# The end of layer 0 by tiles of 128 tokens

## What is computed

```python
for l in range(DEPTH):
    ...
    hl = rmsnorm(x, norm1_w[l]) * (1 + sc1) + sh1
    hc = rmsnorm(ctx, norm1_w[l]) * (1 + csc1) + csh1
    ...
    e_idx, e_w = route_hierarchical(toks, ...)      # two experts a token
    ffn = moe_ffn(toks, e_idx, e_w, w_gate, w_up, w_down)
    x = x + g2 * ffn[:n_lat].reshape(b, t, d)
    if not last:
        ctx = ctx + cg2 * ffn[n_lat:].reshape(ctx.shape)
```

## Time and profile before

| | us |
|---|---|
| median of 3 runs | 3706.56 |
| lowest, highest | 3702.25, 3714.03 |
| the profiled execution, device time | 3713.84 |
| its span, first to last instruction | 3711.9 |
| TensorE busy | 3456.7 (93%) |
| VectorE, ScalarE, Pool busy | 1631.2, 1048.9, 677.6 |
| mean granted TensorE clock | 0.978 of full |

### The profile page before, as it was taken

The page is one execution under the profiler, slowest core; times in us unless marked ns, Lnnn a source line. Parts: engine busy times, 40 slices in busy tenths (PEclk is TensorE's granted clock), DMA queues, the critical chain, the costliest instruction groups (busy, mean ns, idle before and its releaser), DMA issues. The chain is left out here.

```text
span 3711.9 us, 92740 instructions
## 1 busy us (share of the span) xinstructions
PE 3456.7 (93%) x41758; PEld 1938.9 (52%) x41758; DVE 1631.2 (44%) x2896; ACT 1048.9 (28%) x1844; POOL 677.6 (18%) x583
## 2 busy tenths in 40 slices
PE   6989999999999999999999597998999999999997
PEld 3454444545666666443332345656656666774333
DVE  3584803664766663221000356824256666531111
ACT  2211002504545543111111321104145555420001
POOL 0151200302434332010000002113033333300000
PEclk8999999999999999999999799999999999999998
DMA  5103622341110111359998211833311111268996
GB/s 203 64 5 108 221 68 80 120 136 41 27 36 23 28 34 48 115 205 421 404 393 343 101 46 46 260 113 103 93 27 36 26 31 31 53 225 369 424 424 272
DMA packets 255517, 538.69 MB, mean 145 GB/s; under 512 B 49520, under 2 KB 173696, under 8 KB 222224
## 3 DMA queue, kind: packets, MB, share of 16 engines
q1 hardware_dynamic: 236064, 463.98, 34.3%
q0 software_dynamic: 19056, 68.69, 5.3%
HBM read 514.75 MB, written 17.87 MB: 143 GB/s over the span
## 5 line engine op out<-in xcount | busy, mean ns | idle before, releaser
L1299 PE MATMUL banks<-sb_h,sb_ring 128*128 128x512 f32 (+1 forms) x1344 | 476.4, 513 | 10.1 <-DMA sb_ring<-w_branch 6.5
L1816 PEld LDWEIGHTS banks<-inv 64*64 64x64 f32 x15104 | 290.3, 134 | 170.6 <-issue 168.4
L1299 PEld LDWEIGHTS banks<-sb_h,sb_ring 128*128 128x128 f32 x1344 | 255.5, 191 | 224.0 <-issue 196.6
L1816 PE MATMUL banks<-inv 64*64 64x64 f32 x15104 | 328.5, 221 | 14.3 <-issue 10.6
L1825 PE MATMUL banks<-sb_h,sb_ring 128*128 128x512 f32 (+1 forms) x672 | 329.6, 598 | 6.2 <-DMA sb_ring<-w_in 4.1
L819 PE MATMUL banks<-sb_h,sb_ring 128*128 128x512 f32 x512 | 232.1, 611 | 19.4 <-SPq L241 19.4
L3189 PE MATMUL banks<-gu,xs 128*64 128x512 f32 x768 | 169.5, 594 | 5.1 <-DMA gu<-gu_pairs 4.6
L819 PEld LDWEIGHTS banks<-sb_h,sb_ring 128*128 128x128 f32 x512 | 99.8, 197 | 138.8 <-issue 118.1
L2533 DVE COPY inv<-banks 128x512 f32<-128x512 f32 x144 | 98.9, 691 | 164.9 <-PE banks L1816 164.1
L3341 DVE TENSOR_TENSOR hrow<-hrow,banks 128x256 f32<-128x256 f32 x36 | 15.1, 421 | 355.2 <-ACT hrow L3377 355.2
L1299 PE MATMUL banks<-sb_branch,sb_ring 128*128 128x512 f32 (+1 forms) x512 | 170.9, 487 | 0.0
(11 more groups left out here) (484 smaller groups left out, 5663.8 us busy)
## 6 DMA issues: line engine op xcount, KB each, us to landing
gu<-gu_pairs SPq DMA_DIRECT2D x64, 1536.0 KB, 16.8
gu<-gu_tiles SPq DMA_DIRECT2D x57, 1024.0 KB, 8.4
sb_ring<-w_in SPq DMA_DIRECT2D x24, 2048.0 KB, 9.3
sb_ring<-gu_tiles SPq DMA_DIRECT2D x39, 1024.0 KB, 9.2
vtok<-w_mod POOLq DMA_DIRECT2D x64, 512.0 KB, 5.5
sb_ring<-down_pairs SPq DMA_DIRECT2D x32, 1024.0 KB, 14.7
sb_ring<-w_in SPq DMA_DIRECT2D x58, 512.0 KB, 3.9
sb_ring<-down_tiles SPq DMA_DIRECT2D x25, 1024.0 KB, 8.4
```

The source lines that it names most:

```text
L1299: mm = nc.tensor.matmul(out, left(kt), right(kt), start=kt == 0, stop=kt == KT - 1)
L1816: m = mm(k.bank[bank][H[to], at:at + w], left, right, start=start, stop=True, skip_group_check=True)
```

## The change

`norm_first` goes. What it did moves into the end of `experts_rows` and is done by tiles of 128 tokens:

- After the last product each engine passes the overflow path (`experts_dense`, now with `room` in buffers that are free by then, and `add_out`, which adds straight to `k.x`). VectorE then raises `dense_done`; POOL's gathers wait for that and no longer for `ws.used`.
- SP asks for the next slabs after the last gather has landed (`got[3]`), no longer when the ring comes free.
- ScalarE preloads the table "natural_log". Then for each tile: weighed rows (ScalarE), mixed (VectorE), turned (TensorE); VectorE updates `k.x` straight from PSUM (`join`, no copy to `k.acc`); ScalarE squares; TensorE sums; ScalarE makes the root (`root_and_affine`); POOL multiplies the whole tile by it (VectorE for tile 3); ScalarE scales and shifts feature tiles 0 to 3, VectorE 4 to 7.
- The semaphores of the new part are cleared with those of the weight stream, after the block.

```diff
@@ inverse_root: the count of the wait is an argument
-    act.wait_ge(done, 1)
+    act.wait_ge(done, count)
@@ experts_rows, SP
-            ask_next_slabs(k, sp, [(ws.used, ws.total - 2), (ws.used, ws.total)])
             sp.wait_ge(s.stored, 16)
+            sp.wait_ge(ws.used, ws.total)
+            weights(sp)
+            for t in range(NT - 1):
+                sp.wait_ge(got[t], 32)
+            ask_next_slabs(k, sp, [(got[NT - 1], 32), (got[NT - 1], 32)])
@@ POOL
-            pool.wait_ge(ws.used, ws.total)
+            pool.wait_ge(s.dense_done, 1)
             for t in range(NT):
                 for c, buf in enumerate((first, second)):
                     nc.gpsimd.indirect_dma_start(buf[:, t], None, k.d.rows_out, index(t, c), bounds_check=EXPERTS * C - 1, oob_is_err=False)\
                         .then_inc(got[t], 16)
+            for t in range(NT - 1):
+                pool.wait_ge(e.tail_root, 2 * t + 2)
+                nc.gpsimd.tensor_tensor(token_tile(k.h, t), token_tile(k.x, t), rinv[:, t % 2].unsqueeze(1).to_broadcast([P, KT, P]), ALU.mult)\
+                    .then_inc(e.scaled, 1)
@@ VectorE
+            dense_sums(v)
+            v.sem_inc(s.dense_done, 1)
+
+            def mix(t):
+                v.wait_ge(e.weighed, t + 1)
+                nc.vector.scalar_tensor_tensor(first[:, t], second[:, t], rt.share[:, t, 1:2], first[:, t], ALU.mult, ALU.add).then_inc(e.mixed, 1)
+
+            def join(t):
+                for half in range(2):
+                    v.wait_ge(e.back, 2 * t + half + 1)
+                    for f in range(4):
+                        m = 4 * half + f
+                        x = k.x[:, m, P * t:P * t + P]
+                        ins = nc.vector.scalar_tensor_tensor(x, joined(t, half)[:, P * f:P * f + P], k.mod[:, 40 + m, P * t // LC:P * t // LC + 1], x,
+                                                             ALU.mult, ALU.add)
+                    ins.then_inc(e.joined, 1)
+
+            def affine(t):
+                v.wait_ge(e.scaled, t + 1)
+                h, c = token_tile(k.h, t), P * t // LC
+                for m in range(4, KT):
+                    nc.vector.tensor_scalar(h[:, m], h[:, m], k.nscale[:, 0, m, c:c + 1], k.mod[:, m, c:c + 1], ALU.mult, ALU.add)
+
+            mix(0)
             for t in range(NT):
-                v.wait_ge(s.weighed, t + 1)
-                nc.vector.scalar_tensor_tensor(first[:, t], second[:, t], rt.share[:, t, 1:2], first[:, t], ALU.mult, ALU.add).then_inc(s.mixed, 1)
+                if t + 1 < NT:
+                    mix(t + 1)
+                join(t)
+                if t:
+                    affine(t - 1)
+            t = NT - 1
+            v.wait_ge(e.tail_root, 2 * t + 2)
+            v.wait_ge(e.scaled, t)
+            nc.vector.tensor_tensor(token_tile(k.h, t), token_tile(k.x, t), rinv[:, t % 2].unsqueeze(1).to_broadcast([P, KT, P]), ALU.mult).then_inc(e.scaled, 1)
+            affine(t)
@@ ScalarE (take_back goes)
+            silus(act)
+            nc.scalar.preload_act_table_set("natural_log")
+
+            def weigh(t):
+                act.wait_ge(got[t], 32)
+                ac(first[:, t], first[:, t], ACT.Copy, scale=rt.share[:, t, 0:1]).then_inc(e.weighed, 1)
+
+            def squares_of(t):
+                if t >= 2:
+                    act.wait_ge(e.tail_sum, t - 1)
+                for half in range(2):
+                    act.wait_ge(e.joined, 2 * t + half + 1)
+                    ac(sq_tail[:, t % 2, 4 * half:4 * half + 4], token_tile(k.x, t, half), ACT.Square).then_inc(e.squared, 1)
+
+            def root_and_affine(t):
+                act.wait_ge(e.tail_sum, t + 1)
+                if t >= 2:
+                    act.wait_ge(e.scaled, t - 1)
+                inverse_root(k, act, rinv[:, t % 2], tail_sums[t % 2][:, 0:P], e.tail_root, 2 * t + 1)
+                act.wait_ge(e.scaled, t + 1)
+                h, c = token_tile(k.h, t), P * t // LC
+                for m in range(4):
+                    ac(h[:, m], h[:, m], ACT.Identity, bias=k.mod[:, m, c:c + 1], scale=k.nscale[:, 0, m, c:c + 1]).then_inc(e.affine, 1)
+
             act.wait_ge(s.last, 1)
+            weigh(0)
+            weigh(1)
             for t in range(NT):
-                act.wait_ge(got[t], 32)
-                ac(first[:, t], first[:, t], ACT.Copy, scale=rt.share[:, t, 0:1]).then_inc(s.weighed, 1)
+                squares_of(t)
+                if t + 2 < NT:
+                    weigh(t + 2)
                 if t:
-                    take_back(t - 1)
-            take_back(NT - 1)
+                    root_and_affine(t - 1)
+            root_and_affine(NT - 1)
@@ TensorE: turns of tile t, then the sums of tile t - 1
+            dense_products(pe)
+            def join(t):
+                pe.wait_ge(e.mixed, t + 1)
+                for half in range(2):
+                    if t >= 2:
+                        pe.wait_ge(e.joined, 2 * (t - 2) + half + 1)
+                    for f in range(4):
+                        m = turn(joined(t, half)[:, P * f:P * f + P], first[:, t, 512 * half + P * f:512 * half + P * f + P], ident)
+                    m.then_inc(e.back, 1)
+            def sums(t):
+                pe.wait_ge(e.squared, 2 * t + 2)
+                if t >= 2:
+                    pe.wait_ge(e.tail_root, 2 * (t - 2) + 1)
+                for f in range(KT):
+                    m = mm(tail_sums[t % 2][:, 0:P], const(k, "ones"), sq_tail[:, t % 2, f], start=f == 0, stop=f == KT - 1)
+                m.then_inc(e.tail_sum, 1)
+            for t in range(NT):
+                join(t)
+                if t:
+                    sums(t - 1)
+            sums(NT - 1)
```

More of the change, by code:

```diff
@@ L498, in sums @@
                     v.wait_ge(s.out_done, e * KT + (m + 1))
-                    nc.vector.tensor_tensor(k.acc[:, m, t0:], k.acc[:, m, t0:], k.bank[4 + m % 4][:, 0:n], ALU.add).then_inc(s.out_bank_free, 1)
+                    add_out(m, k.bank[4 + m % 4][:, 0:n]).then_inc(s.out_bank_free, 1)
             v.wait_ge(s.out_bank_free, 4 + EXPERTS * KT)
     return weights, products, silus, sums
[L505 to L547, removed]
-            inverse_root(k, act, rinv[:], sums, s.root)
-            for m in range(KT):
-                act.wait_ge(s.normed, m + 1)
-                for c in range(2):
-                    x = k.h[:, m, LC * c:LC * c + LC]
-                    nc.scalar.activation(x, x, ACT.Identity, bias=k.mod[:, m, c:c + 1], scale=k.nscale[:, 0, m, c:c + 1]).then_inc(s.affine, 1)
@@ L3239, in _, with later_semaphores @@
             scatter(R - 1)
+def later_semaphores(k, names):
+    for sem in _cleared:
+        k.nc.release_semaphore(sem)
+    _cleared[:] = []
+    sems = namedtuple("LaterSemaphores", names)(*(k.nc.alloc_semaphore(name=f"{n}_later{k.layer}") for n in names.split()))
+    k.later = list(sems)
+    return sems
 def experts_rows(k, rt, tok, ws):
@@ L3248, in experts_rows @@
     with ExitStack() as st:
-        s = st.enter_context(phase(nc, FRONT + " onehot turned turned_in rows_turned gu_done silu mul d_done ys_in weighed mixed back acc_in"))
+        s = st.enter_context(phase(nc, FRONT + " onehot turned turned_in rows_turned gu_done silu mul d_done ys_in dense_done"))
+        e = later_semaphores(k, DENSE + " weighed mixed back joined squared tail_sum tail_root scaled affine")
         def sb(name, *shape):
@@ L3271, in experts_rows, with token_tile, joined, add_out @@
         pieces = [(i, j, (P * i + 32 * j) // C) for i in range(ROUNDS) for j in range(4)]
+        held, wide_x = ws.gu[:].rearrange("p j e c -> p (j e c)"), xs[:].rearrange("p j kt c -> p (j kt c)")
+        at = [sum(DENSE_ROOM[1:i]) for i in range(1, 5)]
+        room = [wide_x] + [held[:, at[i]:at[i + 1]] for i in range(3)] + [row[:, 0, 0:TT]]
+        sq_tail = wide_x[:, 0:2 * D].rearrange("p (j f c) -> p j f c", j=2, f=KT)
+        rinv = hrow[:, 0, 0:2 * P].rearrange("p (j c) -> p j c", j=2)
+        tail_sums = k.bank[4:6]
+        def token_tile(a, t, half=None):
+            return a[:, slice(0, KT) if half is None else slice(4 * half, 4 * half + 4), P * t:P * t + P]
+        def joined(t, half):
+            return k.bank[2 * (t % 2) + half]
+        def add_out(m, out):
+            for c in range(2):
+                x = k.x[:, m, LC * c:LC * c + LC]
+                ins = nc.vector.scalar_tensor_tensor(x, out[:, LC * c:LC * c + LC], k.mod[:, 40 + m, c:c + 1], x, ALU.mult, ALU.add)
+            return ins
+        weights, dense_products, silus, dense_sums = experts_dense(k, room, e, l, rt.flag, 0, add_out)
         def third(g, n):
@@ L3608, in program @@
         k.nc, k.d = nc, d
+        k.later = []
         k.first = [st.enter_context(nc.semaphore(f"first_slab{h}")) for h in range(2)]
@@ L3628, in program @@
                 modulation(k)
-            else:
-                norm_first(k, flag)
             with ExitStack() as ssd:
```

41 lines of the change are left out of this document (20 added, 21 removed).

## The result

Before: 3706.8 us, median of 6 runs (3702.25 to 3714.03). After: 3732.07 us, median of 6 runs (3725.57 to 3737.51). The ratio is 1.0062, with a 95% interval from 1.0052 to 1.0072: 25 us slower, where 3.4 us were forecast and 3719 was the upper end of the range. The profiled execution of after took 3730.1 us with a span of 3728.2 (before 3713.84 and 3711.9), so the profiles lie 16.3 us apart.

A forecast was written before the change was run, and what follows sets the result against it. The serial tail between layers 0 and 1 was taken as the bound, TensorE working 17.40 of 56.90 us. Terms -5.1, +8.2 and +0.3 gave +3.4 us, from median 3706.56 to 3710.0; range 3699 to 3719 (91%).

The forecast's parts named there:

- Slabs asked later: Start of the tail: last stores land in 2.3 us instead of 7.4, so the first gather starts earlier, -5.1 us.
- The new tail: First gather to last scale and shift: tiles run one behind the other through VectorE, ScalarE, Pool; 46.7 to 54.9, +8.2 us.
- The boundary: Remaining phase boundary behind the tail: clears more semaphores on SP before its first ask, +0.3 us.
- A switch stalls longer: Rival, 6%: seven table switches in the tail each stall another 1.28 us, costing 9.0, for 3719.0 us.
- One load serves Ln and Exp: Rival, 7%: one table serves both in the tail's roots, all seven switches go, -9.1, for 3700.9 us.
- Later slabs free nothing: Rival, 10%: last stores land late for another cause, the first gather stays put, +5.1, for 3715.1 us.
- The rest of the program: Outside the changed tail: 5% left for a change by code placement or the run spread, without a size.

The follow-up runs named there:

- paired order: Changed kernel with 32 jumped-over products between the layers, scale and shift written later, Ln of two tiles ahead of their Exp: 3702.67 us, ratio 0.9959.
- slabs_early: Changed kernel with 32 jumped-over products between the layers, both slabs asked ahead of the gathers again: 3720.58 us, ratio 1.0014.
- after with 40 skipped: Changed kernel with 40 never-executed products (160 TensorE instructions) in layer 0's overflow path: 3724.39 us against 3718.08, ratio 1.0014.
- before with 24 skipped: Kernel before the change with 24 never-executed products (96 TensorE instructions) in layer 0's overflow path: 3731.57 us against 3718.08, ratio 1.0033.

## Why the prediction was wrong

Point by point:

- **Slabs asked later, -5.1.** Right in mechanism, a little large: from the last store to the first gather 3.79 us instead of 8.47, -4.7. The stores land in 2.3 us, but the gather starts 1.5 us behind that, not 1.0; its absolute time, 2043.59 for 2043.8, fits by luck, since the last store came 0.66 us earlier. Undone alone, it costs 5.4. SP asks at 2059.16 (forecast 2059.3), and the next phase waits for no slab.
- **The new tail, +8.2.** Right in mechanism and size: 54.4 us from the gather against 46.7, +7.7. The Pool product, which no row of before showed, took 2.33 to 2.34 us; 2.37 had been taken from the earlier trace rows. The handoffs to Pool and back were 0.08 (Exp ends at 2078.03, Pool starts at 2078.11) and 0.03 us (2080.45 to 2080.48), for 0.09 and 0.13. Seven loads lie on the path. TensorE's sums were mis-sized: sixteen records and 3.78 us, not eight and 2.0, since a product with the ones stands twice in the trace where a turn stands once. They cost nothing on the loop because they lie beside VectorE's join and ScalarE's affine, which is the cover named. In the paired order, where that cover is thinner, they cost 1.02 us.
- **The boundary, +0.3.** 1.69 us from the last scale and shift (2097.97) to the first product (2099.66), 1.48 before: +0.2.
- **The sum of the three.** -4.7, +7.7 and +0.2 give the measured 3.2 for 3.4.
- **A switch stalls longer.** It doesn't: the load at 2076.43 ends at 2077.71 and Exp starts at 2077.72. By the figure of the Trainium skill (ScalarE: Activation LUTs, "What ACT_TABLE_LOAD costs") the seven switches would have cost 9.5 us more, and the tail would have been 64 us; the trace disagrees.
- **One load serves Ln and Exp.** It doesn't: every Exp has its own, 2076.43 among them.
- **Later slabs free nothing.** It falls, by slabs_early's 5.4 us.
- **The rest of the program.** Here the prediction failed: "5% is left for a change of the rest of the program by code placement or the run spread". The step gave the mechanism no size and kept it out of the range, as if 5% of chance could stand for a cost. In its place the runs showed a cost of the change itself: the 96 instructions move the borders of TensorE's pieces in the RWKV phase of layer 1, more fetches come late there, and the phase takes 18.2 us longer, more than the whole 16.3 by which the profiles differ. What could have been worked out ahead: the change adds 24 products with the ones to TensorE's program (32 sums for 8), the waits of TensorE in the RWKV phase of before already hold 18.4 us of "issue", in stalls of up to 1.4 us that no other engine causes, and before's page has the same line of 337 instruction packets. With the sizes now measured, a change of TensorE's instruction count ahead of that phase may move this kernel from some -5 to +19 us by this alone, and a range of 3699 to 3719 was too narrow by the upper part of it.

The Trainium skill (Runtime: NRT & Kernel Launch, "Instruction fetch mechanics") calls a border's cost mostly hidden. By number the traces agree: of some 120 borders in the phase 4 to 21 stop TensorE for 0.7 us or more. But the phase differs by up to 30 us between the places.

**What stays open.** That the placement of code, modulo 256 TensorE instructions, decides on 10 to 30 us of this phase is shown, by never executed code in both kernels; that the stops are late fetches is shown by their places and by the packets ahead of them. That a fetch is late because weight traffic lies in front of it is a reading of the traces: it covers 28 of the 29 stops over 1.8 us (at least 1.3 us of traffic each), but only some 70% of those over 0.7, and no run moved the traffic. And the parts measured on their own, some 5 us for the edit (after with 40 skipped) and 13 for the placement (before with 24 skipped), make 18 to 19, where the medians differ by 25 (19 to 27 by the interval); where the rest comes from, another part of the program or another chip, was not found.

## To carry to other kernels

Before you cost an edit in a kernel with a long stretch of short products on TensorE, count the instructions that it adds to TensorE's program ahead of that stretch, and give their placement a term in the range, of the size of the "issue" stalls that the stretch shows. When a change comes out otherwise than its own stage says, cut both spans at common events first; then pad the program with code that is jumped over, and judge the edit at equal placement. Number TensorE's records, too: here all longer stops without a releaser shared one number modulo 256. In a tail that runs by tiles around several engines, the order written for each engine is worth more than the operations: here it took 11.6 us off the same work, where saving four of seven table loads took 1.9.

## What the hardware showed that I had not expected

- TensorE's time for unchanged code depends on the number of instructions ahead of it, with a shift of 256 neutral and one of 128 costing 19 us in 3716 (0.5%); the phase of 15233 products took 607 to 637 us by it. In fourteen traces all 151 stops of that phase by "issue" of 0.7 us or more lie at borders of 256 records, 1.2 to 1.6 us behind the landing of a 16 KB packet.
- Behind a stall of 2.51 us inside dense products lie 5 us at the granted clock 0.50, in which 89 products were done for 173. In after's phase 10.7 us more of idle time came with 7.5 us more of busy time.
- Three stores of 256 KB land in 2.3 us by themselves and in 7.4 to 8.2 us beside two transfers of 2 MB, though the slabs were asked on another queue.
